# Gates stage of a hybrid S5, SSD and attention trunk: small products in one burst behind each slice, both heads together, weight halves two slices ahead

## The reference

```python
h = rmsnorm(x, norm_w[i])
proj = h @ w_in[i]
...
y_s5 = s5_mixer(...) * silu(s5_gate)      # diagonal complex state space model, GLU
y_ssd = ssd_mixer(...)                    # 16 heads; exp(segsum(a)) * (C B^T), then @ (x * dt)
y_att = window_attention(...)             # 16 query heads of 64, 4 key heads, softmax with sinks
branches = einsum('blnw,nwd->blnd', ys, w_branch[i])
gates = sigmoid(merge_logits).reshape(bsz, L, 3, D_MODEL)
merged = sum(gates * branches, axis=2)
x = x + merged @ w_out[i]
```

## Time and profile before

| what | us |
|---|---|
| median of 3 runs (2064.08 to 2070.47) | 2066.89 |
| the profiled execution | 2067.61 |
| its span, first to last instruction | 2065.9 |
| gates stage of layer 1, 360.65 to 728.44 | 367.79 |
| gates stage of layer 2, 1379.28 to 1748.16 | 368.88 |
| PE busy over the span | 1937.2 (94%) |
| DVE busy over the span | 1552.1 (75%) |
| ACT busy over the span | 1043.9 (51%) |

### The profile page before, as it was taken

The page is one execution under the profiler, slowest core; times in us unless marked ns, Lnnn a source line. Parts: engine busy times, 40 slices in busy tenths (PEclk is TensorE's granted clock), DMA queues, the critical chain, the costliest instruction groups (busy, mean ns, idle before and its releaser), DMA issues.

```text
span 2065.9 us, 36752 instructions
## 1 busy us (share of the span) xinstructions
PE 1937.2 (94%) x12268; PEld 1710.0 (83%) x12268; DVE 1552.1 (75%) x2141; ACT 1043.9 (51%) x1334; POOL 680.2 (33%) x816
## 2 busy tenths in 40 slices
PE   4889999999999998999988999999999999989998
PEld 4889999777777797889978899987777777978898
DVE  6758999888888857666567599988888878566654
ACT  5343444767666654333343344457566766533343
POOL 3036666435343000002410566665343330000034
PEclk9999999999999999999999999999999999999999
DMA  6444444444444445665644444444444444556656
GB/s 258 145 150 145 164 157 157 157 161 163 155 145 164 147 162 221 224 235 203 203 150 143 150 164 164 161 157 158 156 164 145 154 158 153 179 215 226 244 185 211
DMA packets 57898, 359.04 MB, mean 174 GB/s; under 512 B 6928, under 2 KB 7440, under 8 KB 18960
## 3 DMA queue, kind: packets, MB, share of 16 engines
q1 hardware_dynamic: 54480, 345.03, 47.2%
q0 software_dynamic: 1600, 7.85, 1.1%
q10 hardware_dynamic: 1696, 4.72, 0.6%
HBM read 340.27 MB, written 19.40 MB: 174 GB/s over the span
## 4 chain that ended last, share of the span: by engine, by line
PE 52%; DVE 18%; issue 16%; ACT 7%; DMA 3%; POOL 2%; DVEq 1%; ACTq 0%; POOLq 0%; SPq 0%
PE mm L1484 8%; PE mm L1486 8%; PE mm L1485 8%; PE mm L1525 7%; PE mm L1526 7%; PE mm L1527 7%; DVE prod L890 5%; DVE state L890 3%; ACT w_hi L590 3%; DVE w_lo L886 2%; DMA raw<-in_stream 2%; DVE wst L1148 1%; PE b L1600 1%; ACT L657 1%; PE bs L1612 1%
## 5 line engine op out<-in xcount | busy, mean ns | idle before, releaser
L590 ACT ACTIVATE w_hi<-raw 128x2048 fp32r<-128x2048 f32 x299 | 571.4, 1912 | 673.8 <-DMA raw<-in_stream 666.7
L886 DVE TENSOR_TENSOR w_lo<-raw,w_hi 128x2048 fp32r<-128x2048 f32 x299 | 695.3, 2326 | 182.2 <-ACT w_hi L590 175.9
L1484 PE MATMUL mm<-h_lo,w_hi 128*128 128x256 f32 x2240 | 649.3, 290 | 5.9 <-DVE h_lo L890 5.5
L1485 PE MATMUL mm<-h_hi,w_lo 128*128 128x256 f32 x2240 | 637.6, 285 | 0.0
L1486 PE MATMUL mm<-h_hi,w_hi 128*128 128x256 f32 x2240 | 637.4, 285 | 0.0
L1484 PEld LDWEIGHTS mm<-h_lo,w_hi 128*128 128x128 f32 x2240 | 434.2, 194 | 12.6 <-DVE h_lo L890 6.2
L1485 PEld LDWEIGHTS mm<-h_hi,w_lo 128*128 128x128 f32 x2240 | 433.8, 194 | 2.3 <-issue 1.0
L1486 PEld LDWEIGHTS mm<-h_hi,w_hi 128*128 128x128 f32 x2240 | 433.3, 193 | 0.0
L1525 PE MATMUL mm<-w_lo,h_hi 128*128 128x512 f32 x768 | 322.7, 420 | 15.8 <-ACT gt L704 15.8
L1527 PE MATMUL mm<-w_hi,h_lo 128*128 128x512 f32 x768 | 302.3, 394 | 0.0
L1526 PE MATMUL mm<-w_hi,h_hi 128*128 128x512 f32 x768 | 301.5, 393 | 0.0
(11 more groups left out here) (285 smaller groups left out, 2823.1 us busy)
## 6 DMA issues: line engine op xcount, KB each, us to landing
raw<-in_stream SPq DMA_DIRECT2D x300, 1024.0 KB, 4.8
gscr<-gt SPq DMA_DIRECT2D x48, 256.0 KB, 5.9
gin<-gscr SPq DMA_DIRECT2D x24, 512.0 KB, 5.7
x_old<-out POOLq DMA_DIRECT2D x2, 2048.0 KB, 10.8
out<-proj ACTq DMA_DIRECT2D x8, 512.0 KB, 6.2
proj<-in_x SPq DMA_DIRECT2D x4, 512.0 KB, 6.6
par<-in_params POOLq DMA_DIRECT2D x2, 759.0 KB, 4.7
cst<-in_consts SPq DMA_DIRECT2D x1, 1029.0 KB, 16.6
```

Of the source, the lines that this page charges most:

```text
L590: e.activation(w_hi[:, j % RAW, :], raw[:, j % RAW, :], ACT.Copy).then_inc(hi_done, 1)
L886: e.tensor_tensor(w_lo[:, j % RAW, :], raw[:, j % RAW, :], w_hi[:, j % RAW, :].bitcast(F32), ALU.subtract).then_inc(lo_done, 1)
L1484: e.matmul(out, whi, xlo, start=start, stop=False)
L1485: e.matmul(out, wlo, xhi, start=False, stop=False)
```

## The change

`gates` becomes a function: it is written out once with `head` true and then stands in a loop of three passes. All small products stand behind a slice, none in the middle. The two heads of a pair are issued together: `A1` writes head 0 to `b7` and head 1 to `b5`, `ys` and `A3` alternate between the heads; `ex`, `pr` and `small` have a copy for each head, and the scores are made in `pr` itself. The last steps of a pair's attention (`pt`, `A3`, `yatt`, rounding and difference) are carried into the next pair's steps 0 to 2, and those of the last pair into the stage behind. In the gates stage ACT and DVE now make the halves of slice s+`NEAR` (2 ahead), and both do it at another place: ACT behind its small work of the step (decays, `inv_sqrt`, exponentials, scalings, gate evictions), DVE behind the reading of the step's results. In the stage behind, two slices' halves are made at n = 0, and the squares for the SSD norm begin one slice later.

```diff
-RAW, LEAD, SPLIT = 4, 3, 2
+RAW, LEAD, NEAR, SPLIT = 4, 3, 2, 2
...
-                with e.Fori(0, 4) as I:
+                def pt_out(back):
+                    for h in range(2):
+                        W.wait(MP, f"A2_{h}", back)
+                        W.wait(TP, "A3", 1)
+                        MA.mark(e.activation(pt[:, h], (b5, b7)[h][:, 0:384], ACT.Copy), f"pt{h}")
+
+                def att_hi(i):
+                    W.wait(TV, "yatt")
+                    W.settle()
+                    TA.mark(e.activation(ys[:, bass.ds(i + AG, 1), :], proj[:, bass.ds(i + Q, 1), :], ACT.Copy), "end")
+
+                def gates(I, head):
                     nb = start(L, N_GATE, I, 12)
...
                         for t in range(6):
                             s = 6 * c + t
+                            tail = not (head and c == 0)
+                            if t == 0 and tail:
+                                W.tail(L, I * 2 + (c - 1))
+                                pt_out(1)
+                            if t == 0:
+                                W.wait(MP, "q_ss", 1)
+                                MA.mark(e.activation(tq[:], proj[:, bass.ds(i + Q, 1), :], ACT.Square), "q_sq")
+                                W.wait(MV, "conv3")
+                                MA.mark(e.activation(tt[:], xc[:], ACT.Tanh, scale=0.5), "xc_tanh")
+                                sum_decays(0)
+                            if t == 1:
+                                inv_sqrt(MA, "q", qh[:], rq[:], rv[:], lambda: W.wait(MV, "q_v"))
+                                if tail:
+                                    att_hi(I * 2 + (c - 1))
+                            if t == 3:
+                                head_exp(0)
+                                sum_decays(1)
                             if t == 4:
+                                head_exp(1)
+                                att_exp(0)
                                 att_exp(1)
                             if t == 5:
-                                pt_out(1)
+                                att_norm(0)
+                                att_norm(1)
+                                W.wait(MV, "yz", 1)
+                                MA.mark(e.activation(tz[:], proj[:, bass.ds(i + Z, 1), :], ACT.Tanh, scale=0.5), "tz")
+                                if tail:
+                                    W.wait(TV, "yatt")
+                                MA.mark(e.activation(ta[:], proj[:, bass.ds(i + AG, 1), :], ACT.Tanh, scale=0.5), "ta")
                             if s % QUAD == QUAD - 1:
                                 gate(s // QUAD, 0)
                                 gate(s // QUAD, 1)
-                            hi(nb, s + LEAD)
-                            if t == 0:
-                                W.wait(MP, "q_ss", 1)
-                                MA.mark(e.activation(tq[:], proj[:, bass.ds(i + Q, 1), :], ACT.Square), "q_sq")
-                            if t == 4:
-                                att_norm(1)
-                            if t == 1:
-                                inv_sqrt(MA, "q", qh[:], rq[:], rv[:], lambda: W.wait(MV, "q_v"))
-                            if t == 0:
-                                W.wait(MV, "conv3")
-                                MA.mark(e.activation(tt[:], xc[:], ACT.Tanh, scale=0.5), "xc_tanh")
-                                sum_decays(0)
+                            if not (head and s == 0):
+                                hi(nb, s + NEAR)
                             if s == 0:
                                 sines(0)
                                 sines(1)
-                            if t == 2:
-                                head_exp(0)
-                                sum_decays(1)
-                            if t == 3:
-                                att_exp(0)
-                                head_exp(1)
-                                att_norm(0)
-                            if t == 4:
-                                pt_out(0)
-
-                                MA.mark(e.activation(tz[:], proj[:, bass.ds(i + Z, 1), :], ACT.Tanh, scale=0.5), "tz")
-                                MA.mark(e.activation(ta[:], proj[:, bass.ds(i + AG, 1), :], ACT.Tanh, scale=0.5), "ta")
-                            if t == 5:
-                                W.wait(MV, "yatt")
-                                W.settle()
-                                MA.mark(e.activation(ys[:, bass.ds(i + AG, 1), :], proj[:, bass.ds(i + Q, 1), :], ACT.Copy), "end")
...
+                gates(0, True)
+                with e.Fori(0, 3) as J:
+                    gates(e.snap(J + 1), False)
 
                 W.last_tile(L)
+                pt_out(0)
                 W.wait(SV, "s5g2")
-                W.wait(MV, "end")
-                W.wait(MP, "A3_1")
+                W.wait(MV, "yz")
...
+                    if n == 0:
+                        hi(nb, NEAR)
                     hi(nb, n + LEAD)
                     if n == 1:
+                        att_hi(7)
+                    if n == 2:
+                        W.wait(TV, "end")
                         LA.mark(e.activation(g2_hi[:], proj[:, 0:BT, :], ACT.Copy), "g2_hi")
...
+                            if t == 2:
+                                if tail:
+                                    att_lo(I * 2 + (c - 1))
                                 W.wait(MP, "xT")
-                                W.wait(MP, "ys1", 1)
+                                W.wait(MP, "ys", 1)
                                 W.wait(MG, "cur1")
                                 MV.mark(tt_(xdt[:], b6[:, 0:256].rearrange("p (a h d) -> p a h d", a=2, h=2),
                                             cc[:, 20:24].rearrange("p (a h) -> p a h", a=2).unsqueeze(3).broadcast_to([P, 2, 2, 64]),
                                             ALU.mult), "xdt")
+                                W.wait(MV, "qn")
+                                MV.mark(tt_(qh[:], qn[:], C("cos"), ALU.mult), "q_c")
                             if t == 3:
+                                W.wait(MP, "q_rot")
+                                MV.mark(tt_(rq[:], b7[:, 256:512], C("sin"), ALU.mult), "q_s")
+                                W.wait(MV, "q_s")
+                                MV.mark(tt_(qh[:], qh[:], rq[:], ALU.add), "qh")
+                                st_make(0)
+                            if t == 4:
                                 att_scores(0)
-                            if s == 4:
-                                states(0)
-                            if s == 10:
-                                inputs(3)
-                            if t == 4:
+                                att_scores(1)
+                                st_make(1)
+                            if t == 5:
+                                att_sum(0)
                                 att_sum(1)
-                            if s == 10:
-                                scan(3)
-                            if t == 5:
+                                W.wait(MP, "ys")
+                                W.wait(MG, "cur4")
+                                MV.mark(e.scalar_tensor_tensor(xc[:], xc[:], cc[:, 27:28], ps_ssd, ALU.mult, ALU.add), "yv")
                                 W.wait(MA, "tz")
...
-                                out()
-                            lo(nb, s + LEAD)
+                                W.wait(MV, "zb")
+                                MV.mark(e.scalar_tensor_tensor(slot(Z), xc[:], 0.5, tz[:], ALU.mult, ALU.mult), "yz")
+                            if not (head and s == 0):
+                                lo(nb, s + NEAR)
                             if t == 0:
                                 W.wait(MA, "xc_tanh")
                                 MV.mark(e.scalar_tensor_tensor(xc[:], tt[:], 1.0, xc[:], ALU.add, ALU.mult), "xc")
-                            if t == 2:
-                                W.wait(MV, "qn")
-                                MV.mark(tt_(qh[:], qn[:], C("cos"), ALU.mult), "q_c")
-                                st_make(0)
-                                W.wait(MP, "q_rot")
-                                MV.mark(tt_(rq[:], b7[:, 256:512], C("sin"), ALU.mult), "q_s")
-                                W.wait(MV, "q_s")
-                                MV.mark(tt_(qh[:], qh[:], rq[:], ALU.add), "qh")
...
+                            if t == 1:
+                                newton(MV, "q", qh[:], rq[:], rv[:])
+                                W.wait(MP, "q_rot", 1)
+                                MV.mark(e.scalar_tensor_tensor(qn[:], slot(Q), PR("q_norm"), qh[:], ALU.mult, ALU.mult), "qn")
...
                                 back(1)
                                 inputs(1)
                             if s == 5:
                                 scan(1)
                                 forth(1)
+                                states(1)
...
-                        def ssd_y(h):
```

(68 more changed lines are left out.)

180 lines of the change are left out of this document (69 added, 111 removed).

## The result

The changed kernel takes 2244.89 us (median of 4 runs, 2240.93 to 2249.42) against 2067.8 for the kernel before: a ratio of 1.0858, 95% interval 1.0831 to 1.0886, so 8.6% slower. Forecast were 2242 us. The profiled execution has a span of 2243.1 us, 177.2 more than before.

What follows compares the result with a forecast made beforehand. PE and DVE were both taken as near full, with DVE's waits for ACT's halves setting the price: 2067.61 + 160.1 (gates stages) + 12.8 (stage behind) = 2240.5, plus 1.5 for the clock, 2242 us; range 2170 to 2295.

Steps and rivals of the forecast that it cites:

- The mechanism: Gates stages: ACT's half behind small work that answers DVE's same step makes DVE idle; +160.1 us.
- The waits slice by slice: Gates group: DVE's waits under the new order, listed per slice plus gelu, summing to 33.6 us.
- Slice 5: DVE's waits in slices 5 and 11: scalings and `tz` 1.3 twice, then the half 1.05 and 2.25; 5.9 us.
- slice 3: Gates group: half behind the second gate eviction, itself behind the slice's end; 11.1 against 8 of DVE's work, wait 3.2 us.
- the rival of the clock: Gates stages: waits drop PE to half clock, 3.4 us there lose 1.7; 2255 or 2320 us; over 2295, chance 0.06.
- DVE's work: Gates group: does not shrink, 78.8 us, the busy time and half a microsecond of links.
- DVE busy unchanged near 309: Sign for the gates stages: DVE's busy time stays near 309 us a stage.
- The groups: Gates stage: first group 105.6 us, second 112.4, then two of 115.2 each; stage 448.4.
- PE's waits: Gates group: PE waits some 30 us, eight waits above 2 us; its savings of 3.8 are lost in them.
- PE busy lower: Sign for PE: its busy time falls, with waits for `qn`, the evictions, `pn` and `xc`.
- The stage behind: Per layer: `A3` 1.0, PE's wait for `pt` 1.8, squares 3.7; together 6.4, so +12.8 us, between 2 and 18.
- PE sets the pace: Rival, gates stages: DVE's waits under 10.8 us a group, so PE's 82.6 decides; 2006 us, chance 0.07.

Runs made afterwards that it cites:

- step 1 alone: Changed kernel with ACT's weight half ahead of the small work at step 1 only (slices 1 and 7), behind it elsewhere; 2217.7 us, ratio 1.075.
- DVE's S5 work moved: Changed kernel, ACT's half first every step, plus DVE's S5 work before Newton's steps, squares a slice earlier, extra halves of the stage behind earlier; 2058.46 us.
- Half first: Changed kernel with ACT's weight half ahead of its small work in every step of the gates stage; 2074.96 us, ratio 1.0038 to the kernel before.
- the last version: Kernel of 2058.46 us with DVE's gates loop written out and ACT's sines moved from slice 6 to 8 and 0 to 2; 2018.69 us, ratio 0.9761.

## Why the prediction was right

- **The mechanism** is shown from both sides: taken away, 170 us come back; put into the kernel before in one step, some 55 us are lost. That the time came out within 3 us is in part luck, since errors of both signs stand in the sum, as the next points show.
- **The waits slice by slice.** Predicted for slices 0, 1, 3, 4, 6, 7, 10: 3.3, 5.9, 3.2, 2.6, 3.3, 5.4, 2.6. Measured in the third group: 3.17, 6.01, 5.78, 2.59, 3.17, 5.14, 2.59. Slice 5: 1.05 before its half, measured 0.89; slice 11: 2.25, measured 2.03. One term is mis-sized, slice 3, by 2.6 us. Its half stands behind the eviction at the end of slice 3, and PE had just waited for `qn` and fallen to half clock (window and timeline of PE):

```profile
608.40:618.50 10.10, 5.67 (x15) 4.19 (x16) 9.74 (x17) 1.76 (x5) 4.19 (x11) 0.50 0.22 91
...
612.18 1.22 PE L1761 MATMUL b<-qn,cst 128*128 128x256 f32 x2 [5.81 <-DVE qn L1349]
```

  Slice 3 took 622.78 - 615.78 = 7.0 us in place of 5.5, and from the end of `qn` to its start 3.7 in place of 3.0: 2.2 of the 2.6 us. The other 0.4 is DVE's work in that time, 7.6 for 8. So the rival of the clock had the right place and a price too low: 1.7 a group there, 2.2 here.
- **DVE's work** was the term that hid this. I had 78.8 us a group, with half a microsecond of links (from a busy time of 78.27 in a window slightly longer than that of the earlier trace rows, which has 78.23); the window says 76.37 busy. In the group of the earlier trace rows its half took up to 3130 ns, median 2286; in the third group after it took 2293 at most. Idle time is 116.18 - 76.37 = 39.8 against 33.6 + 2.8 = 36.4 predicted. Work 2.4 too high and waits 3.4 too low gave 115.2 against 116.18. What stretches the half in the kernel before was not tested, but the trace has a lead: its three long ones, 2.56, 2.48 and 3.13 us, started at 504.89, 513.29 and 520.00, while an instruction of POOL had 0.40, 0.33 and 0.98 us still to run. "DVE busy unchanged near 309" was wrong: 300.3 up to the same point. Its wait for `w_hi` was forecast at some 25 us a group and is 31.
- **The groups**: 105.6, 112.4, 115.2, 115.2 predicted; 109.5, 113.4, 116.2 and 110.8 measured (the last 112.8 up to the first matmul of the stage behind). The first was forecast 4 us too short: its wait at slice 1 was 9.1 us, not 5.9. The last was forecast too long: DVE's work there is 73.0 us, 3.4 less than in the third, and the forecast had one figure for all.
- **PE's waits**: 5.6 before `q_rot`, 4.5 for the eviction at slice 8, 3.2 before `A2`; measured at most 5.8, 4.1 and 2.8. The sum was too high: in the third group PE's waits are 23.7 us, not some 30, and four are above 2 us, not eight. PE's busy time was too low in its place: "PE busy lower" holds for its share of the stage alone, the time rose from 353.8 to 366.5 us up to the same point, at a clock of 0.92 in place of 1.00.
- **The stage behind**: 1.8 for `pt` and 3.7 for the squares. Waits of PE there:

```profile
820.18 0.87 PE L1678 MATMUL by<-pt,vcur 128*64 128x256 f32 x8 [1.56 <-ACT pt L701]
...
836.41 1.44 PE L1809 MATMUL b<-ssq,cst 128*128 128x256 f32 x4 [3.67 <-ACT ssq L843]
```

  Together with `A3`, taken at 1.0 as predicted, 6.2 a layer of the 6.4; outside the stages the profile is 10.9 us longer for the 12.8, and the stages 166.3 for the 160.1.
- **The rivals.** "PE sets the pace" had its condition right: under some 10.8 us of DVE waits a group PE decides. It needed another order of ACT, DVE's loop written out and the sines moved to come near, and gives 2018.7 there, not 2006.

## What to carry to other kernels

Where two engines hand work to each other in strict order, ask for each step which work feeds the full engine and which only answers it; what feeds it stands first, and how far ahead it runs must leave the transfer time to land. A full engine in the page does not say that it sets the pace: laying one period out in order of time, with durations from rows, named the price to 2% (174 us against 177), and afterwards the direction of the moves. Its sizes can be far off where another wait takes over: step 1 alone was laid out at twice what it gave, DVE's S5 work moved at nearly five times.

## What the hardware showed that I had not expected

**The turn of DVE's gates loop took 2.8 to 5.8 us.** From its jump back to its next instruction DVE stood 2.8 to 3.1 us in the kernels before and after, 3.2 to 5.8 in those two slices ahead with ACT's half first everywhere or at step 1; the same loop turns in 0.3 us on ACT and POOL. Windows from the jump to DVE's next instruction, last column GB/s. The kernel before:

```profile
455.80:458.70 2.90, 2.90 (x15) 2.41 (x14) 0.35 (x1) 2.21 (x2) 1.61 (x4) 1.00 0.40 78
```

Half first, two turns:

```profile
541.70:546.70 5.00, 4.75 (x26) 3.25 (x25) 0.31 (x1) 2.94 (x4) 0.00 (x0) 1.00 0.65 202
636.60:640.00 3.40, 1.73 (x9) 1.15 (x8) 0.32 (x1) 2.93 (x4) 0.00 (x0) 1.00 0.53 148
```

Step 1 first:

```profile
577.60:583.30 5.70, 4.03 (x22) 3.01 (x23) 0.35 (x1) 1.18 (x3) 1.53 (x4) 1.00 0.59 197
```

The length goes with when SP issued the slice's load. In the kernels before and after it was issued 0.7 to 0.9 us after the jump; in "step 1 first" 0.7 us before it (5.7 us). In "half first" a load stands 4.1 us before the jump with two spills of gates 3.5 and 2.9 before it (5.0 us), or 5.5 with the spills 4.7 and 4.1 before it (3.4). Every one of these windows has one or two packets of an instruction queue (q14) among its DMA traffic, and the gates stage has 21 of them in the kernel before, 13 with DVE's loop written out: the turn fetches code. That this fetch queues behind a load is my reading of the order and was not tested by itself. The price of the jump was tested: written out, the row of the turn falls from 9.4 to 0.2 us, and 15 us are gone. The Trainium skill (Runtime: NRT & Kernel Launch, Instruction fetch mechanics) says that a jump out of the fetched window makes the sequencer fetch by DMA before it goes on; the packets in these windows agree with that.

**The overlap of row halves needs no alternation**, 0.87 us for 768 columns in either order.

**Waits of PE cost again in its clock.** In the changed kernel the granted clock is 0.92 over the gates stage, where it was 1.00 before and is 1.00 in the last version; with the same large matmuls PE is busy 12.7 us longer there, up to the first matmul of the stage behind.
